# The router's logits with the weights stationary, the choice made on logits, and the first gather ahead of the branch

## The chip, the core and the metric

One core of a Trainium2 chip runs the whole program in one launch. The metric is device microseconds of one execution. Everything is fp32. Matmuls of the big layers run on operands in the fp32r format, split in two parts; the router and the experts use plain fp32 operands.

## The reference, cut to what matters

The program is two layers of three sublayers (four feed-forward, one pooling, one attention), a hybrid mixer, and at the end a mixture of experts for 256 tokens of 1024 channels. Only the last part is touched:

```
def hier_moe(h, w_rg, b_rg, w_re, b_re, w_eg, w_eu, w_ed):
    xt = h.reshape(n_tok, dm)                       # 256 x 1024
    lg = xt @ w_rg + b_rg                           # 4 groups
    grp = jnp.argmax(lg, axis=-1)
    p_grp = take_along_axis(softmax(lg), grp)
    le = (xt @ w_re + b_re).reshape(n_tok, 4, 8)    # 8 experts of each group
    le = le of the group grp
    top_p, top_i = lax.top_k(softmax(le), 2)
    gate = top_p / sum(top_p) * p_grp
    expert = grp * 8 + top_i
    ...
    yb = (silu(xb @ w_eg[e]) * (xb @ w_eu[e])) @ w_ed[e]   # per expert, on its tokens
    return sum over a token's two experts of gate * yb
```

## The kernel before, in words

Weights come from DRAM in one stream of chunks of 1.5 MB into a ring of six slots. SyncE issues chunk n as soon as chunk n-6 is used (semaphore `chunk_used`, line 236 in the loop). Each engine's program is written out by hand, and semaphores alone order the engines. TensorE's helper `mm` (line 398) issues all matmuls; an fp32 matmul stands in the trace as two instructions with a weight load each, a transpose as one.

The stages are in order: pre-norm of the experts' input, which leaves `H` (channels on partitions, 8 tiles of 128 channels x 256 tokens, VectorE line 2122); the router; a branch; the experts.

The router before. TensorE: for each half of the tokens (t) and each channel tile (k), a matmul with the tile of `H` as weights (128x128) and 36 columns of router weights as moving data, 16 matmuls in all, so the logits lie with tokens on partitions. Then 16 transposes of `H` (line 1225) into psA, which ScalarE copies to `HTOK` (line 1902), tokens on partitions. VectorE: the bias, then steps on little tiles, each waiting for the one before (`link`). `first_max` is five such steps (largest, equal, times a falling weight, largest, equal) and gives the first largest entry as one-hot. It finds the group, masks the experts' logits, subtracts the largest, and waits for ScalarE's exponentials (lines 1905, 1906, behind the copy in ScalarE's order). On the exponentials it finds the two experts `O1` and `O2`, and their sum `ASG` (line 2748) lets TensorE count, by three matmuls, each token's place in its expert's list. Meanwhile VectorE works out the gates (lines 2750 to 2757), then the places `POS` (line 2760), the longest list (lines 2761 and 2764, with TensorE's transpose 1234 between), and writes it to `most` (line 2765).

All engines read `most` and branch: to `sparse()` if no expert has over 64 tokens (it is taken here), else to `dense()`. In `sparse()` experts go in 16 pairs. A pair's selection matrix `SEL` is two compares on VectorE (line 2241); TensorE gathers the pair's tokens with it from `HTOK` (`gather`, 16 matmuls, in two halves of four channel tiles), VectorE copies each half to `XE` (line 2254); `select` turns `SEL` and picks the gates (line 1277 and two matmuls of 2 columns); then the gate and up matmuls, 64 instructions of 512 columns, read the ring and begin to free its slots. Within a pair TensorE goes on with the transposes of line 1305, the next pair's select and gather, and the down matmuls.

Filled into waits of TensorE are matmuls without use, `idle(n, w)`, each two instructions of w columns. During the router nine transfers of 0.5 MB, issued from ScalarE (line 1985), put the last three chunks of the first pair into free parts of `mem`, and one chunk goes to the ring slot that the router's weights leave.

Of the kernel before, what the change touches and what calls it, by code (L numbers as in the profile page):

```python
# [18 lines left out]
P = 128  # L19
S = 256  # L20
# [44 lines left out]
for _n, _c in [("c", 8), ("ada_b", 144), ("norm_g", 96), ("pool_b", 8), ("pool_scale", 8),  # L65
               ("norm_mix", 8), ("norm_ffn", 8), ("b_gate", 24), ("q_norm", 2), ("kv_norm", 1),
               ("conv_a", 12), ("conv_g", 48), ("qk_gain", 4), ("out_gain", 1), ("pe", 32),
               ("b_rt", 36), ("a_log", 4), ("dt", 4)]:
    COLS[_n] = (NCOL, NCOL + _c)
    NCOL += _c  # L70
# [7 lines left out]
def build(nc, stream, cols_d, ident_d, x_d, masks_d, out_d):  # L78
    ctx = ExitStack()
    with ctx:  # L80
# [304 lines left out]
        HTOK, XE = tiles(16, 2, D), tiles(18, 1, P)  # L385
        EARLY_AT = (0, 1, 2, 3, 23, 25, 14, 15, 20)
# [8 lines left out]
        def _(pe):  # L395
# [817 lines left out]
            def router():  # L1213
                c = BASE["out"] + 2
                for t in range(TT):
                    for k in range(KT):
                        pe.wait_ge(h_ready, 8 * 7 + k + 1)
                        a = 2 * SLOT + k * 36
                        last = mm(psS[:, 0, t * 36:(t + 1) * 36], H[:, k, t * P:(t + 1) * P],
                                  chunk(c, a, a + 36), start=(k == 0), stop=(k == KT - 1))  # L1220
                last.then_inc(chunk_used, 1)

                for t in range(TT):
                    for k in range(KT):
                        last = nc.tensor.transpose(psA[:, 2 * t + k // 4, (k % 4) * P:(k % 4 + 1) * P],
                                                   H[:, k, t * P:(t + 1) * P], ident)
                last.then_inc(sem("rt_htok"), 1)

                pe.wait_ge(sem("rt_asg"), 1)
                mm(psS[:, 0, 0:E], before, ASG[:, 0, :], start=True, stop=True)  # L1230
                mm(psS[:, 0, E:2 * E], before, ASG[:, 1, :], start=False, stop=False)
                mm(psS[:, 0, E:2 * E], ones, ASG[:, 0, :], start=False, stop=True).then_inc(sem("rt_cnt"), 1)
                pe.wait_ge(sem("rt_max1"), 1)
                nc.tensor.transpose(psS[0:1, 0, 256:256 + P], blk(22)[:, 128:129], ident).then_inc(sem("rt_max1t"), 1)
# [27 lines left out]
            def sparse():  # L1262


                def gather(r, p):
                    pe.wait_ge(sem("sp_sel"), r * 6 + (p + 1))
                    for b in range(2):
                        for k in range(4 * b, 4 * b + 4):
                            for t in range(TT):
                                last = mm(psG[:, b, (k % 4) * P:(k % 4 + 1) * P], HTOK[:, t, k * P:(k + 1) * P],  # L1270
                                          SEL[:, p % 2, t, :], start=(k % 4 == 0 and t == 0), stop=(t == 1))
                        last.then_inc(sem("sp_ga"), 1)
# [66 lines left out]
                def step(r, p):  # L1339
# [4 lines left out]
                    if not isinstance(r, int) or p < NP - 1:  # L1344
                        select(r, p + 1)
                        gather(r, p + 1)
                    down(r, p)

                pe.wait_ge(sem("htok_out"), 1)
                gather(0, 0)  # L1350
# [11 lines left out]
            def dense():  # L1362

                t0 = 4 * NF
                for t in range(TT):
# [12 lines left out]
                pe.wait_ge(sem("htok_out"), 1)  # L1378
# [88 lines left out]
        def _(ac):  # L1467
# [432 lines left out]
            def router():  # L1900
                ac.wait_ge(sem("rt_htok"), 1)
                A(HTOK.rearrange("p t (b n) -> p (t b) n", b=2), psA[:, :, :], ACT.Copy).then_inc(sem("htok_out"), 1)
                ac.wait_ge(sem("rt_max"), 1)

                A(blk(24)[:, 256:264], blk(24)[:, 256:264], ACT.Exp)
                A(blk(24)[:, 128:192], blk(24)[:, 128:192], ACT.Exp).then_inc(sem("rt_exp"), 1)
# [91 lines left out]
        def _(ve):  # L1998
# [232 lines left out]

            def sparse():

                def selection(r, p):

                    if p >= 2 or not isinstance(r, int):
                        ve.wait_ge(sem("sp_st"), r * 2 + (p - 1))
                    for t in range(TT):
                        a = t * E + 2 * p
                        pos = blk(22)[:, 64 + a:66 + a] if isinstance(r, int) else blk(22)[:, bass.ds(r * 4 + (64 + a), 2)]  # L2240
                        last = V.tensor_tensor(SEL[:, p % 2, t, :].rearrange("p (e s) -> p e s", e=2),
                                               iota[:, None, :].to_broadcast([P, 2, CAP]),
                                               pos[:, :, None].to_broadcast([P, 2, CAP]), ALU.is_equal)
                    last.then_inc(sem("sp_sel"), 1)
# [4 lines left out]

                def xe(r, p):  # L2250

                    for b in range(2):
                        ve.wait_ge(sem("sp_ga"), r * 4 + (2 * p + b + 1))
                        V.tensor_copy(XE[:, 4 * b:4 * b + 4, :].rearrange("p k s -> p (k s)"), psG[:, b, :])\
                            .then_inc(sem("sp_xe"), 1)
# [8 lines left out]
                def step(r, p):  # L2264
                    hidden(r, p)
                    if not isinstance(r, int) or p < NP - 1:
                        xe(r, p + 1)
# [4 lines left out]
                selection(0, 0)  # L2272
                selection(0, 1)
                xe(0, 0)
# [102 lines left out]
            def hybrid():  # L2377
# [312 lines left out]
                add_acc()  # L2690

# [4 lines left out]

            def router():
                w = blk(24)
# [370 lines left out]
```

## Time and profile before

| | us |
|---|---|
| median of 3 runs | 1949.6 (1947.92 to 1955.89) |
| the profiled execution | 1949.58, its span 1947.5 |
| TensorE matmul busy | 1832.8 (94% of the span) |
| VectorE busy | 976.4 (50%) |
| ScalarE busy | 684.1 (35%) |
| DMA, mean over the span | 248 GB/s |

Busy shares are averages over stages with different limits, and say little of a stretch of 30 us. The line numbers in rows are those of the kernel before; a matmul's line is mostly the helper's, so its tiles tell which it is: `psS<-ring,H` are the logits, `psA<-cst,H` the transposes, `psG<-mem` the gather, `psG<-cst` the idle matmuls, `psS<-ring,mem` the gate and up matmuls.

### The profile page before, as it was taken

How to read it: one execution, taken by the hardware profiler on the slowest of the kernel's cores; microseconds unless marked ns; L12 is line 12 of the kernel's file. 1: busy time of each engine (PE TensorE's matmuls, PEld its weight loads, DVE VectorE, ACT ScalarE, POOL GpSimd, SP SyncE). 2: the span in 40 equal slices, each digit the busy share in tenths (PEclk: the TensorE clock that was granted, in tenths of full speed). 3: DMA queues.
4: the chain of work that ended last, by engine and by line, in shares of the span. 5: the costliest groups of instructions: out<-in, count | busy, mean ns of one | idle time of the engine just before them, and what ended most of it. 6: DMA issues, size and time to landing. Idle time of an engine off the chain costs nothing.

```text
span 1947.5 us, 33027 instructions
## 1 busy us (share of the span) xinstructions
PE 1832.8 (94%) x13777; PEld 1505.1 (77%) x13777; DVE 976.4 (50%) x1406; ACT 684.1 (35%) x1049; POOL 21.6 (1%) x14
## 2 busy tenths in 40 slices
PE   7999999999999988999999899988888999999997
PEld 5999989999999976799998799877774543444433
DVE  3988668886855446355457775456522111111111
ACT  3444444444443335344445333455411110110101
POOL 0000000000000000000000021000000000000000
PEclk9999999999999999999998899989998999999999
DMA  9999529995664411534532222522354999999997
GB/s 394 425 365 341 190 102 374 343 346 195 270 249 173 184 55 66 195 140 184 192 132 98 98 98 98 211 95 103 138 200 189 413 426 426 424 425 425 425 425 297
DMA packets 46045, 483.46 MB, mean 248 GB/s; under 512 B 5105, under 2 KB 5233, under 8 KB 7153
## 3 DMA queue, kind: packets, MB, share of 16 engines
q1 hardware_dynamic: 44496, 476.09, 61.8%
q10 hardware_dynamic: 1440, 5.77, 0.8%
q8 instruction: 88, 1.44, 0.3%
q14 instruction: 21, 0.16, 0.0%
HBM read 480.79 MB, written 1.05 MB: 247 GB/s over the span
## 4 chain that ended last, share of the span: by engine, by line
PE 42%; DMA 8%; DVE 4%; ACT 2%; issue 1%; DVEq 0%; SPq 0%; ACTq 0%
PE psG L398 25%; PE psA L398 9%; DMA ring<-stream 8%; PE psS L398 6%; DVE parts L2089 1%; ACT parts L1505 0%; DVE mem L2403 0%; ACT mem L1866 0%; PE psS L1305 0%; DVE sg L2424 0%; DVE mem L2173 0%; PE psS L1159 0%; ACT mem L1516 0%; DVE mem L2668 0%; DVE mem L2645 0%
## 5 line engine op out<-in xcount | busy, mean ns | idle before, releaser
L398 PE MATMUL psG<-parts 128*128 128x256 f32 x6016 | 772.7, 288 | 13.0 <-issue 9.0
L398 PEld LDWEIGHTS psG<-parts 128*128 128x128 f32 x6016 | 748.1, 195 | 30.4 <-issue 24.4
L398 PE MATMUL psA<-parts 128*128 128x256 f32 x2368 | 303.2, 284 | 1.8 <-DVE parts L2260 1.6
L398 PEld LDWEIGHTS psA<-parts 128*128 128x128 f32 x2368 | 290.7, 192 | 18.1 <-issue 15.6
L398 PE MATMUL psS<-ring,mem 128*64 128x512 f32 (+1 forms) x1028 | 232.1, 598 | 20.5 <-DMA ring<-stream 17.3
L2027 DVE TENSOR_TENSOR parts<-ring,parts 128x2048 fp32r<-128x2048 f32 x80 | 183.1, 2289 | 117.6 <-ACT parts L1481 117.3
L398 PEld LDWEIGHTS psS<-ring,mem 128*64 128x64 f32 (+1 forms) x1028 | 72.7, 138 | 175.5 <-issue 132.2
L1481 ACT ACTIVATE parts<-ring 128x2048 fp32r<-128x2048 f32 x80 | 153.1, 1914 | 89.1 <-PE psA L398 88.5
L2018 DVE SCALAR_TENSOR_TENSOR mem<-ring,silc,mem 128x1536 f32<-128x1536 f32 (+1 forms) x98 | 138.8, 1417 | 2.5
L2089 DVE TENSOR_TENSOR parts<-ring,parts 128x1024 fp32r<-128x1024 f32 x76 | 95.2, 1257 | 88.8 <-ACT parts L1505 87.6
L1505 ACT ACTIVATE parts<-ring 128x1024 fp32r<-128x1024 f32 x76 | 79.9, 1053 | 139.4 <-PE psG L398 139.4
L2248 DVE TENSOR_TENSOR mem<-mem,psS 128x512 f32<-128x512 f32 x16 | 11.0, 687 | 234.0 <-ACT mem L1931 234.0
L1592 ACT ACTIVATE sg<-psG 128x256 f32<-128x256 f32 x88 | 33.8, 384 | 212.8 <-PE psG L398 212.6
L398 PE MATMUL psG<-ring,mem 128*64 128x512 f32 x480 | 106.3, 595 | 0.7 <-ACT mem L1933 0.7
L2030 DVE TENSOR_TENSOR parts<-ring,parts 128x1024 fp32r<-128x1024 f32 x80 | 97.4, 1218 | 0.0
L1931 ACT ACTIVATE mem<-psS 128x512 f32<-128x512 f32 x16 | 9.6, 598 | 233.8 <-PE psS L398 233.8
L398 PE MATMUL psG<-mem 128*128 128x128 f32 (+3 forms) x624 | 81.1, 312 | 5.1 <-ACT mem L1876 2.9
L1482 ACT ACTIVATE parts<-ring 128x1024 fp32r<-128x1024 f32 x80 | 83.3, 1042 | 0.0
L398 PEld LDWEIGHTS psG<-ring,mem 128*64 128x64 f32 x480 | 33.0, 137 | 62.7 <-issue 60.1
L2191 DVE TENSOR_TENSOR act<-sg,psG 128x256 f32<-128x256 f32 x88 | 37.0, 421 | 87.4 <-ACT sg L1592 84.3
L398 PEld LDWEIGHTS psG<-mem 128*128 128x128 f32 (+2 forms) x624 | 68.4, 189 | 12.8 <-issue 7.2
L1926 ACT ACTIVATE parts<-psG,mem 128x512 fp32r<-128x512 f32 x32 | 22.0, 687 | 147.7 <-PE psG L398 147.7
(351 smaller groups left out, 1537.9 us busy)
## 6 DMA issues: line engine op xcount, KB each, us to landing
ring<-stream SPq DMA_DIRECT2D x300, 1536.0 KB, 9.0
mem<-stream ACTq DMA_DIRECT2D x9, 512.0 KB, 7.2
X<-x_in SPq DMA_DIRECT2D x1, 1024.0 KB, 18.0
ring<-stream SPq DMA_DIRECT2D x1, 1024.0 KB, 22.3
mem<-masks ACTq DMA_DIRECT2D x1, 1024.0 KB, 4.8
x_out<-X SPq DMA_DIRECT2D x4, 256.0 KB, 2.9
ring<-stream SPq DMA_DIRECT2D x1, 512.0 KB, 23.9
cst<-consts SPq DMA_DIRECT2D x1, 304.0 KB, 2.9
```

What stands on the lines that cost most here:

```text
L398: return nc.tensor.matmul(out, lhsT, rhs, start=start, stop=stop, skip_group_check=True)
L1481: A(WG[f % 2][:, 0, :], chunk(c, 0, 2 * SLOT), ACT.Copy).then_inc(sem("hi_gu"), 1)
L1482: A(WD[t % 3][:, 0, :], chunk(c, 2 * SLOT, CHUNK), ACT.Copy).then_inc(sem("hi_dn"), 1)
L1505: A(WS[s % 3][:, 0, :], chunk(c, a, a + SLOT), ACT.Copy).then_inc(sem("slot_hi"), 1)
L1592: A(sg[:, t % 2, :], psG[:, t % 2, 0:S], ACT.Silu).then_inc(sem("silu_ready"), 1)
L1926: A(YS[:, 0, h * 512:(h + 1) * 512], psG[:, h, :], ACT.Copy, scale=GSL[:, p % 2:p % 2 + 1])\
L2018: ins = V.scalar_tensor_tensor(out, w[:, q], silc[:, k:k + 1], out, ALU.mult, ALU.add)
L2027: V.tensor_tensor(WG[f % 2][:, 1, :], chunk(c, 0, 2 * SLOT), WG[f % 2][:, 0, :], ALU.subtract).then_inc(sem("lo_gu"), 1)
L2030: V.tensor_tensor(WD[t % 3][:, 1, :], chunk(c, 2 * SLOT, CHUNK), WD[t % 3][:, 0, :], ALU.subtract).then_inc(sem("lo_dn"), 1)
L2089: V.tensor_tensor(WS[s % 3][:, 1, :], chunk(c, a, a + SLOT), WS[s % 3][:, 0, :], ALU.subtract).then_inc(sem("slot_lo"), 1)
L2191: V.tensor_tensor(act[:, f % 2, :], sg[:, f % 2, :], psG[:, f % 2, S:2 * S], ALU.mult).then_inc(sem("hidden"), 1)
L2248: V.tensor_tensor(HACT, HSIL, psS[:, 1, :], ALU.mult).then_inc(sem("sp_act"), 1)
```

## The change

Logits: the router's weights (36 columns) are stationary and `H` moves (256 columns), so the logits come out with groups and experts on partitions and tokens along the row. VectorE adds the bias there (`LGX`, 36x256), and TensorE turns the result back by two transposes of 128 tokens. The 16 transposes of `H` are spread: seven between the logits of the tiles, five behind them, four behind the two turned logits.

Choice: the experts are found on the logits, not on their exponentials, with -1e30 on those of other groups. `ASG` no longer needs ScalarE. The gates use exp of the difference of the two best logits, and are worked out behind both first selections. ScalarE loads its table for exp by a dummy activation ahead of the copy.

Ahead of the branch stand now: the selections of the first two pairs, the first pair's gather and copies. 26 idle matmuls are added, 22 ahead of the counts and 4 behind them. `POS` counts from 1, and the row of positions that it is compared with too, which takes away a step. The 36 memsets of falling weights go to the end of the mixer, ahead of the pre-norm.

```
             def router():                                  # TensorE
-                for t in range(TT):
-                    for k in range(KT):
-                        pe.wait_ge(h_ready, 8 * 7 + k + 1)
-                        last = mm(psS[:, 0, t * 36:(t + 1) * 36], H[:, k, t * P:(t + 1) * P],
-                                  chunk(c, a, a + 36), start=(k == 0), stop=(k == KT - 1))
+                for k in range(KT):
+                    pe.wait_ge(h_ready, 8 * 7 + k + 1)
+                    a = 2 * SLOT + k * 36
+                    last = mm(psS[0:36, 0, 0:S], chunk(c, a, a + 36), H[:, k, :], start=(k == 0), stop=(k == KT - 1))
+                    if k < KT - 1:
+                        token(0, k)
                 last.then_inc(chunk_used, 1)
-                for t in range(TT):
-                    for k in range(KT):
-                        last = nc.tensor.transpose(psA[:, 2 * t + k // 4, (k % 4) * P:(k % 4 + 1) * P],
-                                                   H[:, k, t * P:(t + 1) * P], ident)
+                token(0, KT - 1)
+                for k in range(4):
+                    token(1, k)
+                pe.wait_ge(sem("rt_lgx"), 1)
+                for t in range(TT):
+                    last = nc.tensor.transpose(psS[:, 0, S + t * 36:S + (t + 1) * 36], LGX[:, t * P:(t + 1) * P],
+                                               ident[0:36, 0:36])
+                last.then_inc(sem("rt_lgt"), 1)
+                for k in range(4, KT):
+                    last = token(1, k)
                 last.then_inc(sem("rt_htok"), 1)
+                idle(22, P)
                 pe.wait_ge(sem("rt_asg"), 1)
...
+                idle(4, P)
+                pe.wait_ge(sem("htok_out"), 1)
+                gather_half(0, 0, 0)
                 pe.wait_ge(sem("rt_max1"), 1)
...
+                gather_half(0, 0, 1)
...
             def sparse():                                  # TensorE
-                pe.wait_ge(sem("htok_out"), 1)
-                gather(0, 0)
+                pe.wait_ge(sem("rt_gate"), 1)
                 select(0, 0)
...
             def router():                                  # ScalarE
+                A(blk(24)[0:1, 1000:1001], eps[0:1, 0:1], ACT.Exp)
                 ac.wait_ge(sem("rt_htok"), 1)
...
                 ac.wait_ge(sem("rt_max"), 1)
-                A(blk(24)[:, 256:264], blk(24)[:, 256:264], ACT.Exp)
-                A(blk(24)[:, 128:192], blk(24)[:, 128:192], ACT.Exp).then_inc(sem("rt_exp"), 1)
+                A(EX, EX, ACT.Exp).then_inc(sem("rt_exp"), 1)
...
             def router():                                  # VectorE
-                link(V.tensor_tensor(LGT, rt, b36, ALU.add))
+                link(V.tensor_scalar(LGX, psS[0:36, 0, 0:S], col("b_rt", 0)[0:36], None, ALU.add), "rt_lgx")
+                ve.wait_ge(sem("rt_lgt"), 1)
+                lg = psS[:, 0, S:S + 72].rearrange("p (t c) -> p t c", t=2)
...
+                first_max(lg[:, :, 0:4], W4, OH, 0, 4)
+                link(V.tensor_scalar(OH, OH, 1.0, 1e30, ALU.subtract, ALU.mult))
+                for t in range(TT):
+                    last = V.tensor_tensor(LE[:, t, :].rearrange("p (g e) -> p g e", g=4),
+                                           lg[:, t, 4:36].rearrange("p (g e) -> p g e", g=4),
+                                           OH[:, t, :][:, :, None].to_broadcast([P, 4, 8]), ALU.add)
+                link(last)
+                first_max(LE, W32, O1, 1, 32)
+                link(V.scalar_tensor_tensor(T1, O1, -4e30, LE, ALU.mult, ALU.add))
                 first_max(T1, W32, O2, 4, 32)
                 link(V.tensor_tensor(ASG, O1, O2, ALU.add), "rt_asg")
+                V.tensor_tensor(EXL, lg[:, :, 0:4], Z[:, 0].to_broadcast([P, 2, 4]), ALU.subtract)
+                link(V.tensor_tensor(D2, Z[:, 4], Z[:, 1], ALU.subtract), "rt_max")
+                ve.wait_ge(sem("rt_cnt"), 1)
+                link(V.tensor_tensor(POS, ASG, psS[:, 1, 0:2 * E].rearrange("p (t e) -> p t e", t=2), ALU.mult))
+                selection(0, 0)
+                link(V.tensor_reduce(blk(22)[:, 128:129], blk(22)[:, 64:128], AX.X, ALU.max), "rt_max1")
+                selection(0, 1)
+                ve.wait_ge(sem("rt_exp"), 1)
...
+                xe(0, 0, 0)
                 ve.wait_ge(sem("rt_max1t"), 1)
...
                 link(V.tensor_copy(most[0:1, 0:1], blk(22)[0:1, 130:131]), "rt_flag")
+                xe(0, 0, 1)
```

TensorE from the logits to the first expert matmul, before (`rt_asg` is VectorE's assignment, `rt_max1` its maximum per token, `rt_flag` the value in `most`, `sp_sel` the selection, `sp_xe` the copied gather):

```order
L398 MATMUL psS<-ring,H 128x36 [waits h_ready] x16
L1225 MATMUL psA<-cst,H 128x128 x16
L398 MATMUL psS<-mem,cst 128x32 [waits rt_asg]
L398 MATMUL psS<-mem,cst 128x32 x2
L1234 MATMUL psS<-cst,mem 1x128 [waits rt_max1]
L1458 TENSOR_LOAD most [waits rt_flag]
...
L1459 COMPARE_AND_BRANCH
L398 MATMUL psG<-mem 128x128 [waits sp_sel,htok_out]
L398 MATMUL psG<-mem 128x128 x15
L1277 MATMUL psS<-cst,mem 128x128 x2
```

The same stretch of TensorE in the changed kernel, from the last tile of logits on (`rt_lgx` is the biased logits, `rt_gate` the gates; ahead of these rows seven pairs of a 36x256 matmul and a transpose):

```order
L399 MATMUL psS<-H,ring 36x256 [waits h_ready]
L1220 MATMUL psA<-cst,H 128x128 x5
L1235 MATMUL psS<-cst,mem 128x36 [waits rt_lgx]
...
L1220 MATMUL psA<-cst,H 128x128 x4
L399 MATMUL psG<-cst 128x128 x22
L399 MATMUL psS<-mem,cst 128x32 [waits rt_asg]
...
L399 MATMUL psG<-cst 128x128 x4
L399 MATMUL psG<-mem 128x128 [waits sp_sel,htok_out]
...
L1251 MATMUL psS<-cst,mem 1x128 [waits rt_max1]
L399 MATMUL psG<-mem 128x128 x8
...
L1478 COMPARE_AND_BRANCH
L1296 MATMUL psS<-cst,mem 128x128 [waits rt_gate]
```

The gather has moved ahead of the branch, in two halves around the transpose of the maximum, and 22 idle matmuls stand between the transposes and the counts.

VectorE from the assignment to the first copy of the gather, before (2748 is the assignment, 2760 the places, 2765 the flag, 2241 the selections, 2254 the copies):

```order
L2748 TENSOR_TENSOR mem<-mem 128x64 [waits dve_step]
L2750 TENSOR_TENSOR mem<-mem 128x2 [waits rt_asg]
...
L2752 RECIPROCAL mem<-mem 128x2 [waits dve_step]
...
L2757 TENSOR_TENSOR mem<-mem 128x64 [waits dve_step]
L2760 TENSOR_TENSOR mem<-mem,psS 128x64 [waits rt_cnt,rt_gate]
L2761 TENSOR_REDUCE mem<-mem 128x1 [waits dve_step]
...
L2765 CAST most<-mem 1x1 [waits dve_step]
...
L2820 COMPARE_AND_BRANCH
L2241 TENSOR_TENSOR mem<-cst,mem 128x128 x4
L2254 COPY mem<-psG 128x512 [waits sp_ga] x2
```

And in the changed kernel (2757 is the assignment, 2763 the places, 2257 a selection's compare, 2780 the flag, 2265 the copies):

```order
L2757 TENSOR_TENSOR mem<-mem 128x64 [waits dve_step]
...
L2763 TENSOR_TENSOR mem<-mem,psS 128x64 [waits rt_cnt,rt_max]
L2257 TENSOR_TENSOR mem<-cst,mem 128x128 [waits dve_step]
...
L2765 TENSOR_REDUCE mem<-mem 128x1
L2257 TENSOR_TENSOR mem<-cst,mem 128x128 [waits rt_max1]
...
L2769 TENSOR_REDUCE mem<-mem 128x2 [waits rt_exp]
...
L2775 TENSOR_TENSOR mem<-mem 128x64 [waits dve_step]
L2265 COPY mem<-psG 128x512 [waits sp_ga,rt_gate]
...
L2780 CAST most<-mem 1x1 [waits dve_step]
L2265 COPY mem<-psG 128x512 [waits sp_ga,rt_flag]
...
L2836 COMPARE_AND_BRANCH
```

The gates' steps, which stood between the assignment and the places, now stand behind the selections, and the flag is written between the two copies.

## Rows read from the trace of the kernel before

**Rows 1.** The page's first line, of the whole span.

```profile
span 1947.5 us, 33027 instructions
```

**Rows 2.** Chain of waits in order of time: start us, us, what ran.

```profile
1410.89 27.91 PE psA L398 x128
...
1445.98 6.13 PE psS L398 x32
1452.11 3.48 PE psA L1225 x16
1455.61 1.88 ACT mem L1902
1457.50 1.28 ACT L1905
...
1465.80 0.55 DVEq L2819
...
1467.46 6.64 PE psG L398 x32
...
1474.87 13.98 PE psS L398 x64
...
1584.93 14.16 DMA ring<-stream
...
1702.82 2.03 issue
```

**Rows 3.** Windows: busy time of each engine (count), granted clock, DMA share, GB/s.

```profile
1445.90:1449.00 3.10, 3.02 (x18) 2.36 (x17) 3.09 (x39) 0.00 (x0) 0.00 (x0) 1.00 0.88 301
1449.00:1452.10 3.10, 3.10 (x19) 3.10 (x19) 0.14 (x12) 0.00 (x0) 0.00 (x0) 0.58 1.02 408
1456.00:1458.00 2.00, 0.00 (x0) 0.00 (x0) 0.00 (x0) 1.98 (x2) 0.00 (x0) 0.92 1.03 426
1460.00:1462.00 2.00, 0.00 (x0) 0.00 (x0) 1.75 (x8) 0.00 (x0) 0.00 (x0) 0.50 0.27 111
1462.50:1467.40 4.90, 1.86 (x7) 1.43 (x7) 3.12 (x17) 0.00 (x0) 0.00 (x0) 0.50 0.00 0
1530.00:1543.00 13.00, 13.00 (x64) 4.22 (x60) 0.75 (x1) 0.41 (x1) 0.00 (x0) 1.00 1.02 433
```

**Rows 4.** Timeline of the router: start us, us, engine, instruction [idle before <- releaser].

```profile
1438.40 2.19 PEld L398 LDWEIGHTS psG<-cst 128*128 128x128 f32 x18
...
1443.69 0.55 DVE L2061 RECIPROCAL st<-st 128x64 f32<-128x64 f32 x1 [2.32 <-ACT st L1485]
...
1445.44 3.22 DVE L2122 SCALAR_TENSOR_TENSOR H<-X,cols,psS 128x256 f32<-128x256 f32 x8 [1.20 <-PE psS L398]
...
1448.61 0.49 DVE L2713 MEMSET mem<- 128x1 f32 x32
...
1452.42 0.16 DVE L2723 TENSOR_REDUCE mem<-mem 128x2 f32<-128x8 f32 x1
...
1459.25 0.16 DVE L2743 TENSOR_REDUCE mem<-mem 128x2 f32<-128x8 f32 x1 [3.85 <-ACT mem L1906]
...
1462.28 0.22 DVE L2748 TENSOR_TENSOR mem<-mem 128x64 f32<-128x64 f32 x1
...
1462.56 1.49 PE L398 MATMUL psS<-mem,cst 128*128 128x32 f32 x6 [6.99 <-DVE mem L2748]
...
1464.30 0.22 DVE L2760 TENSOR_TENSOR mem<-mem,psS 128x64 f32<-128x64 f32 x1
...
1465.62 0.14 DVE L2765 CAST most<-mem 1x1 int32<-1x1 f32 x1
...
1466.82 0.90 DVE L2241 TENSOR_TENSOR mem<-cst,mem 128x128 f32<-128x128 f32 x4 [1.06 <-issue]
...
1474.13 0.69 DVE L2254 COPY mem<-psG 128x512 f32<-128x512 f32 x1 [2.19 <-PE psG L398]
```

**Rows 5.** Groups by line and shape, window 1689 to 1720: the gather of a later pair.

```profile
L398 PE MATMUL psG<-mem 128*128 128x128 f32 x32 | 3.8, 278 | 0.0
```

## What the change will do to the time

> **What bounds the kernel now.** The change touches one short stretch, so I read three views: the page's first line for the whole, the chain of waits for what sets the end, and the windows and the timeline for that stretch. The profiled execution took 1949.58 us, its span 1947.5 [rows 1]; 2.1 us lie around the span and stay. Its own time equals the median of the runs (1949.6), so a shift of the span carries over one to one.
>
> The chain [rows 2] shows two regimes. From 1474.87 on the experts run: the first pairs are set by TensorE, but from 1584.93 the chain steps through waits of some 14 us on the weight stream, and the DMA engines are full at 433 GB/s [rows 3]. That looks as if TensorE and VectorE before it did not matter. They do: between the transfers that end at 1460.7 (27% of the window 1460 to 1462) and the first expert matmul the DMA moves nothing (its row reads 0 GB/s) [rows 3]. The ring and the side buffers are full, and nobody frees a slot. The stream starts again only when the first pair's gate-and-up matmuls start; call that moment T0, now 1474.87. Everything after T0 depends on T0 alone, so each microsecond off the router comes off the end.
>
> The stretch from H to T0, 1445.98 to 1474.87 (28.9 us), is a single chain over TensorE, ScalarE and VectorE: 32 logit matmuls 6.13, 16 transposes 3.48, ScalarE's 2048-column copy 1.88, a table load 1.28, then the exponentials; VectorE sits 3.85 us until they are there [rows 2, 4]; then VectorE's small steps, the counts, the branch, 6.64 us of gather. The granted clock is 0.58 from 1449 and 0.50 later [rows 3]: one step from 2.4 to 1.2 GHz, at about 1449.5 (0.5 us at full and 2.6 at half make the mean of 0.58 over 3.1), after 3.5 us of matmuls with 36 moving columns. The gather ran at 1.2 GHz; the same 32 instructions in a later pair take 3.8 us [rows 5].
>
> **The change, part by part.** Pitches that I use: a 128x256 fp32 instruction 27.91/128 = 0.22 us [rows 2]; a 128x128 one at full clock 2.19/18 = 0.12 us [rows 4], the gather 3.8/32 = 0.12 [rows 5], at half clock 16 transposes in 3.48 = 0.22 [rows 2]. One fp32 matmul is two instructions, one transpose is one. VectorE: 64-column steps from 1459.25 to 1462.28 are one short one (0.20) and eleven of (3.03-0.20)/11 = 0.26 [rows 4]; the 8-column ones 0.20.
>
> 1. *Logits.* 16 instructions of 256 columns, 7 transposes between them: 16x0.22 + 7x0.12 = 4.3, and some 0.15 for the last one's tail. VectorE makes H at 3.22/8 = 0.40 a tile [rows 4], faster than the 0.56 that TensorE takes per tile, so H does not gate. End 1450.4, against 1452.1.
> 2. *Bias and turn.* The bias add reads 36x256 from PSUM. Not in the trace; between the small steps (0.2) and the 512-column copy (0.69) [rows 4]; scaled by columns 0.43. Then two transposes and back: 0.06 to start, 0.12 for the first, 0.4 for the second (the counts' 1.49 less five pitches of 0.22), 0.1 back. New: 1450.4+0.05+0.43+0.65 = 1451.5 for the first group step, which now starts at 1452.42. Gain 0.9. The 36 memsets (0.49 for 32 of them, now from 1448.61) would stand in front of this; they move to where VectorE idles 2.32 us before the reciprocal at 1443.69 [rows 4], which hides them. Without that cover they cost 0.6.
> 3. *Choice on logits.* Group 5x0.20, mask 0.20, two adds 0.33, then 1.28, 0.26, 1.28, 0.22 = 4.6 to the assignment: 1456.1, against 1462.50. The wait for ScalarE (3.85) and the group steps of the old softmax are gone. The table load moves behind the last early DMA issue and ahead of the copy, and only ten columns are exponentiated; the result is wanted at 1459.4, about 2.5 us after it is there. If the table had to be loaded twice, it would still be there.
> 4. *Warm-up matmuls.* This is what is late next. Behind the two turned logits stand 4 transposes and idle(22), 44 instructions: 50x0.12 = 6.0 from 1450.9, to 1456.9. The assignment is there at 1456.1, so the counts wait 0.8 in TensorE's queue; VectorE waits for them. Counts start 1456.9, before 1462.56: gain 5.7.
> 5. *Counts and position.* At full clock 5x0.12+0.35 = 0.95 (before 1.49). VectorE's multiply starts 1457.9; before 1464.30, since the gates stood in front. Gain 6.4. The gates' steps move behind both selections, 1.4 us to about 1460.85, just under the first gather half.
> 6. *Selection and gather ahead of the branch.* Multiply 0.26, two selection steps 0.5 (0.90 for four): 1458.7. Here the flag, the branch (VectorE: 1465.76 to 1466.82, 1.06) and the maximum used to stand between; now the gather starts at 1458.75 instead of 1467.46, gain 8.7. idle(4), 0.96, ends at about 1458.6 and hides under it. Halves: 16x0.12 each and one transpose: last issued 1462.7, result 1462.9. Copy 0.69: 1463.6 (before 1474.82). Gain 11.2 on this branch.
> 7. *Branch and select.* VectorE: first copy 1460.9 to 1461.6, flag 1462.1, ahead of the second copy. TensorE then branches and does the first pair's two transposes and four 2-column instructions, 6x0.12. Before, these lay under the copy; now they lie behind. The cost of TensorE's branch is not seen apart: from below 0 beyond the gather; from above the 2.03 us "issue" at the loop's end at 1702.82 [rows 2]; VectorE's own 1.06 [rows 4] is the nearest. With 1.06 counted from 1462.7: 1463.8, select 0.75: T0 = 1464.5. With 0: 1463.7 (the copy ends then); with 2.03: 1465.6.
>
> By the Trainium skill (TensorE: Matmul & The Clock Gate, opening table), TensorE's queue is 64 deep. If its sequencer runs that far ahead, the branch starts at the flag, and T0 would be about 1463.9; no run here shows that.
>
> Sum: 1474.87 - 1464.5 = 10.4, bounds 9.2 to 11.2. Nothing is added behind T0; the stream sees the same full ring (all landed by 1460.7 in either kernel, since the one chunk that the router frees and the nine early ones are the same bytes). 1949.6 - 10.4 = 1939.2.
>
> **Rivals.**
> *The clock drops as before, at about 1449.5, and comes back as before* (for: it is the same transposes, and TensorE waits at the turn; against: 256-column matmuls at 0.22 leave no such gaps as 36-column ones, and idle(22) fills the wait). Then six tiles of logits are done at full, the rest at half: 1451.1. From 1451.6 the 50 instructions run at 0.22 until the clock is back, as it was in the window 1456 to 1458 [rows 3]: some 22 by 1456.4, the other 28 at 0.12 to 1459.8. The counts are 2.9 later than in the forecast and the rest follows: T0 1467.4, time 1942.1.
> *The slower one: the clock falls as the logits start and stays.* Then 16x0.43+7x0.22 = 8.4, logits at 1454.4; the warm-up becomes the bound, 50x0.22 = 11 from 1455.0 to 1466.0, 3.4 later than the counts are now. Counts issued by 1467.3, idle(4) eight more to 1469.1, 33 gather instructions to 1476.4, branch 1.06, select 6x0.22 = 1.3: T0 1478.7, time 1953.4. It decides from the point where the clock falls at 1449.5 and does not return: counts at 1462.6, T0 by the same steps 1475.3, just above today's, since idle(22) at half clock eats all that VectorE saved. Against: from 1445.9 to 1449 the clock was 1.0 [rows 3].
> The row that bears on both: in 1456 to 1458 the clock granted is 0.92 with TensorE empty [rows 3]; it rose after the 16 transposes, which were all it had done since 1452.1.
> The Trainium skill (TensorE: Matmul & The Clock Gate, Part 4: PE-mode transpose) says that transposes don't count as TensorE activity and the full clock doesn't engage for them. By that rule the 17 transposes now mixed in are holes, and the time goes to the two rivals. This trace disagrees with it: 0.92 behind 16 transposes.
> *The gain is swallowed by the stream*: the experts are DMA-bound from 1584.93, so an earlier start only waits longer. For: the 14 us waits. Against: 0 GB/s for the 14 us before T0. It would give 1949.6.
> *A dearer branch*: 2.03 instead of 1.06, T0 1465.6, time 1940.3.
>
> **Numbers.** Forecast 0.72, inside it 1937 to 1941.5; dearer branch 0.12; clock down and back 0.08; swallowed 0.04; slower rival 0.04. The range takes in the forecast, the dearer branch, the clock that returns, and a spread between runs like that of before (1947.92 to 1955.89, mostly upward): 1936.3 to 1944.0. About 0.5% (9.7 us, the line 1939.85) is what a measurement of this kernel tells from no change. The forecast lies only 0.65 inside it: of its 0.72 about 0.48 is faster than the line, and a cheaper branch is in that; of the dearer branch 0.04. Faster 0.52, within 0.46, slower 0.02 (half of the slower rival with an upward run).
>
> **What would show it.** Right: granted clock 1.0 from 1446 to T0; first group step near 1451.5; the counts starting when the idle matmuls end and not when the assignment is ready; the gather in two parts of about 1.9 us; T0 at 1464 to 1465.6; and the whole pattern from T0 to the end unchanged, 1947.5 - 1474.87 = 472.6 us of span behind it. Wrong: a clock of 0.5 in any of it (then step 4 fails first), a branch on TensorE of over 2 us, or a distance from T0 to the end that has grown.

## The result and the profile after

The changed kernel takes 1941.37 us in the median of 11 runs (1937.07 to 1946.73); the kernel before, in 11 runs too, 1951.35 (1947.64 to 1956.3). The ratio is 0.995, 95% interval 0.994 to 0.996, about 10 us. The forecast of 1939.2 started from 1949.6, the median of three runs, so 1.75 of the 2.2 us between forecast and result is the kernel before, and 0.4 the change. The profiled execution took 1942.88 us, its span 1940.9. That is 6.6 us of span less than before [rows 1], not 10, and the stretches tell why.

The chain of waits of the changed kernel, in order of time (start us, us, what ran):

```profile
1413.38 27.91 PE psA L399 x128
...
1448.47 0.62 PE psS L399 x2
...
1456.30 4.91 PE psG L399 x44
1461.21 0.59 PE psS L399 x6
1461.81 0.97 PE psG L399 x8
1462.81 2.02 PE psG L399 x16
1464.94 1.79 PE psG L399 x16
1466.73 0.41 issue
1467.14 0.43 PE psS L1296 x2
1467.57 14.25 PE psS L399 x68
...
1577.90 14.08 DMA ring<-stream
```

Set beside [rows 2] it falls into three pieces. Up to the first logit: 1448.47, before 1445.98, 2.5 us *later*, in code that both kernels share but for the 36 memsets, and all of it is there at the first row already (1413.38, before 1410.89). From there to T0, the first expert matmul, at 1467.84: 19.4 us, before 28.9. From T0 to the end: 1940.9 - 1467.84 = 473.1, before 472.6. So the change is worth 9.5 us in its own stretch, and a pair of executions can show more or less than that, here 6.6, since the start of the logits lies anywhere from 1442.4 to 1452.7 in the thirteen profiles of this study. From T0 to the end they differ by 0.9 at most, so that wandering makes up nearly all of how their spans differ once T0 is taken from the first logit. All comparisons below therefore go by the time from the first logit instruction, written +x; a difference of rounded times can be 0.01 off.

| us from the first logit | before | after | forecast |
|---|---|---|---|
| last logit done, bias add starts | +6.17 | +6.35 | +4.5 |
| first group step | +6.44 | +7.35 | +5.5 |
| assignment done | +16.52 | +11.94 | +10.1 |
| counts start (first weight load) | +16.58 | +12.47 | +10.9 |
| place step | +18.32 | +13.44 | +11.9 |
| gather starts | +21.48 | +14.34 | +12.8 |
| T0 | +28.89 | +19.37 | +18.5 |

The windows of the changed kernel (columns as in [rows 3]):

```profile
1448.40:1454.80 6.40, 6.33 (x24) 2.22 (x25) 2.76 (x8) 1.49 (x2) 0.00 (x0) 1.00 0.95 360
1454.80:1460.90 6.10, 6.10 (x54) 5.89 (x55) 4.68 (x23) 2.07 (x2) 0.00 (x0) 1.00 1.04 428
1460.90:1466.70 5.80, 5.77 (x50) 5.42 (x49) 3.50 (x16) 0.02 (x1) 0.00 (x0) 1.00 0.37 153
1466.00:1468.00 2.00, 1.59 (x15) 1.39 (x15) 0.69 (x1) 0.06 (x1) 0.00 (x0) 1.00 0.00 0
1524.00:1536.00 12.00, 12.00 (x58) 3.86 (x54) 0.17 (x1) 0.00 (x0) 0.00 (x0) 1.00 1.02 434
```

The granted clock is 1.00 all through the router, the DMA still falls silent before T0 (0 GB/s from 1466), and it is full again later, as before [rows 3].

The timeline of the changed kernel, around the logits and around the branch (start us, us, engine, line, operation, then in brackets the idle time ahead and what ended it):

```profile
1448.47 0.14 PEld L399 LDWEIGHTS psS<-H,ring 128*36 128x36 f32 x2 [0.27 <-DVE H L2140]
1448.47 0.62 PE L399 MATMUL psS<-H,ring 128*36 128x256 f32 x2
1449.03 0.14 PEld L1220 LDWEIGHTS psA<-cst,H 128*128 128x128 f32 x1 [0.41 <-issue]
1449.03 0.33 PE L1220 MATMUL psA<-cst,H 128*128 128x128 f32 x1
1449.29 0.14 PEld L399 LDWEIGHTS psS<-H,ring 128*36 128x36 f32 x2
...
1460.18 0.23 DVE L2757 TENSOR_TENSOR mem<-mem 128x64 f32<-128x64 f32 x1
...
1460.94 0.75 PEld L399 LDWEIGHTS psS<-mem,cst 128*128 128x128 f32 x6
...
1461.91 0.22 DVE L2763 TENSOR_TENSOR mem<-mem,psS 128x64 f32<-128x64 f32 x1 [1.24 <-PE psS L399]
...
1465.85 0.14 DVE L2780 CAST most<-mem 1x1 int32<-1x1 f32 x1
1466.83 0.69 DVE L2265 COPY mem<-psG 128x512 f32<-128x512 f32 x1 [0.84 <-PE psG L399]
1467.13 0.20 PEld L1296 LDWEIGHTS psS<-cst,mem 128*128 128x128 f32 x2 [0.59 <-issue]
```

A tile of logits takes 0.81 us (1448.47 to 1449.29), not 0.56: the load for the transpose starts only 0.56 after the pair of matmuls began, when they are nearly through, with the load side idle for 0.41. The branch is the opposite case, cheaper than forecast: from the flag (1465.85 + 0.14 = 1465.99) to TensorE's first instruction behind the branch (1467.13) it is 1.14 us, of which only 0.41 lie behind the last gather matmul (1466.73). The rest ran while the gather was still in TensorE's queue.

### The profile page after: what moved, and what is told of

The parts are those of the page before. It is cut to its first block, busy times and chain, and to the rows that moved or that the text cites. A ratio compares the mean times of both kernels' runs of the same rounds, so it can differ in the third digit from the quotient of the medians.

```text
span 1940.9 us, 33097 instructions
## 1 busy us (share of the span) xinstructions
PE 1835.1 (95%) x13815; PEld 1504.3 (78%) x13815; DVE 975.0 (50%) x1399; ACT 683.8 (35%) x1049; POOL 21.6 (1%) x14
## 4 chain that ended last, share of the span: by engine, by line
PE 40%; DMA 9%; DVE 5%; ACT 2%; issue 1%; DVEq 0%; SPq 0%; ACTq 0%
PE psG L399 24%; DMA ring<-stream 9%; PE psA L399 9%; PE psS L399 6%; DVE parts L2107 1%; DVE mem L2418 1%; ACT parts L1524 0%; ACT mem L1885 0%; PE psS L1324 0%; DVE sg L2439 0%; PE psS L1160 0%; DVE mem L2191 0%; ACT mem L1535 0%; DVE mem L2416 0%; DVE mem L2683 0%
```

## Experiments

**All logits first** (six runs). The transposes leave the gaps between the logits; 28 idle instructions instead of 44.

```
                     last = mm(psS[0:36, 0, 0:S], chunk(c, a, a + 36), H[:, k, :], start=(k == 0), stop=(k == KT - 1))
-                    if k < KT - 1:
-                        token(0, k)
                 last.then_inc(chunk_used, 1)
-                token(0, KT - 1)
-                for k in range(4):
-                    token(1, k)
+                for k in range(5):
+                    token(0, k)
...
-                for k in range(4, KT):
+                for k in range(5, KT):
+                    token(0, k)
+                for k in range(KT):
                     last = token(1, k)
...
-                idle(22, P)
+                idle(14, P)
```

> The changed kernel with its transposes taken out from between the logits: eight logit matmuls first, five transposes behind them, then the two turned logits, then the other eleven transposes, and idle(14) in place of idle(22). Counted from the first logit instruction; the changed kernel has the first group step at +7.35, the counts at +12.47, T0 (first expert matmul) at +19.37 us. Theory A, a matmul behind a transpose and a transpose behind a matmul each wait until the array is empty (0.81 us a tile instead of 0.56): without the seven changes of kind the logits run at 0.22 a piece or at the pace of H, bias add at +3.8, first group step at +4.8 to +4.9, counts at +9.6, T0 at +16.4 to +16.9, so 2.5 to 3 us less than the changed kernel, about 1938.5 where that one has 1941.4. Theory B, a transpose is simply dear by 0.25 us wherever it stands: the eleven transposes behind the turn take 11x0.36 = 4 us, the counts are at about +12, T0 at +19, no gain.

The timeline of this kernel, TensorE and the two VectorE steps that it feeds:

```profile
1446.92 3.64 PE L399 MATMUL psS<-H,ring 128*36 128x256 f32 x16
...
1450.49 0.77 PE L1220 MATMUL psA<-cst,H 128*128 128x128 f32 x5
1450.60 0.48 DVE L2734 TENSOR_SCALAR mem<-psS,cols 36x256 f32<-36x256 f32 x1 [1.00 <-PE psS L399]
...
1451.43 1.42 PE L1220 MATMUL psA<-cst,H 128*128 128x128 f32 x11
1451.61 0.17 DVE L2740 TENSOR_REDUCE mem<-psS 128x2 f32<-128x8 f32 x1 [0.53 <-PE psS L1232]
...
1456.23 0.85 PE L399 MATMUL psS<-mem,cst 128*128 128x32 f32 x6 [0.26 <-DVE mem L2756]
...
1463.03 1.51 PE L399 MATMUL psS<-ring,mem 128*64 128x512 f32 x6
```

Bias add at +3.69, group step +4.70, counts +9.32, T0 +16.12: 3.25 us less than the changed kernel. The sixteen narrow logit instructions run at 0.22 a piece, the transposes in a row at 0.11. Theory B falls: no transpose is dear by itself. The median is 1937.11 us, the ratio to the kernel before 0.9939 (0.9926 to 0.9952). T0 also comes near to another limit here: the DMA still moves 139 GB/s from 1461.5 to 1462.0 and 12 GB/s from 1462 to 1463, so the early transfers have landed only some 1.3 us ahead of T0 (1463.03); in the changed kernel that is some 4.7 us, before 14. The distance from T0 to the end is still 472.4.

**Wide weights** (one run).

```
-                    last = mm(psS[0:36, 0, 0:S], chunk(c, a, a + 36), H[:, k, :], start=(k == 0), stop=(k == KT - 1))
+                    last = mm(psS[:, 0, 0:S], chunk(c, a, a + P), H[:, k, :], start=(k == 0), stop=(k == KT - 1))
```

> The changed kernel with 128 columns of the chunk as the logits' weights instead of 36 (rows 36 to 127 of the result are not used by anything). Theory A (change of kind): the pitch of a tile stays at 0.81 us, T0 at +19.4. Theory C (a narrow weight load of 36 columns keeps the next load from being taken ahead): pitch falls to 0.56, bias add at +4.5 instead of +6.35, T0 at +18.1 or where the idle matmuls let it, since those end then at +10.9.

The timeline of the kernel with wide weights, TensorE and its load side, at its first logits (start us, us, engine, line and operation):

```profile
1448.85 0.30 PEld L399 LDWEIGHTS psS<-H,ring 128*128 128x128 f32 x2 [0.26 <-DVE H L2140]
1448.85 0.70 PE L399 MATMUL psS<-H,ring 128*128 128x256 f32 x2
1449.17 0.14 PEld L1220 LDWEIGHTS psA<-cst,H 128*128 128x128 f32 x1
1449.39 0.27 PE L1220 MATMUL psA<-cst,H 128*128 128x128 f32 x1
1449.39 0.30 PEld L399 LDWEIGHTS psS<-H,ring 128*128 128x128 f32 x2
```

The same order, the same changes of kind, three and a half times the weights: 0.54 a tile (1448.85 to 1449.39). The transpose's load now starts 0.32 after the matmuls did, inside them. Theory A falls, theory C stands. The bias add is at +4.54 (expected +4.5), T0 at +17.42, 1.95 less than in the changed kernel, and earlier than the +18.1 expected. What about a narrow load holds back the wide one no run shows; only 36 and 128 columns were tried.

**Turned by plain matmuls** (one run), in `token`:

```
-                    return nc.tensor.transpose(psA[:, 2 * t + k // 4, (k % 4) * P:(k % 4 + 1) * P],
-                                               H[:, k, t * P:(t + 1) * P], ident)
+                    return mm(psA[:, 2 * t + k // 4, (k % 4) * P:(k % 4 + 1) * P],
+                              H[:, k, t * P:(t + 1) * P], ident, start=True, stop=True)
```

> The changed kernel with the 16 transposes of H done as plain fp32 matmuls against the identity, two instructions each. Theory A (change of kind, matmul to transpose mode): no change of kind is left among them, so a tile takes 2x0.22+2x0.12 = 0.67 us, bias add near +5.3. Theory C (narrow weights): the stall stays, 0.81+0.12 = 0.93 us a tile, bias add near +7.2. The other nine turns cost 9x0.12 = 1.1 us more in either case.

TensorE's load side at this kernel's first logits:

```profile
1444.94 0.14 PEld L399 LDWEIGHTS psS<-H,ring 128*36 128x36 f32 x2 [0.26 <-DVE H L2140]
1445.49 0.30 PEld L399 LDWEIGHTS psA<-cst,H 128*128 128x128 f32 x2 [0.41 <-issue]
1445.91 0.14 PEld L399 LDWEIGHTS psS<-H,ring 128*36 128x36 f32 x2
```

0.97 a tile (1444.94 to 1445.91), bias add at +7.46, T0 +21.52. With no transpose left among the logits the stall is there (load side idle for 0.41), so by this too it goes with the weights' width (36 beside 128) and not with the mode. The size was close to theory C's 0.93.

**No idle matmuls** (one run).

```
-                idle(22, P)
...
-                idle(4, P)
```

> The changed kernel without its 26 idle matmuls. Theory K (they hold the clock): TensorE is empty from about +7.8 to +11.9, the granted clock falls to 0.5 before or in the counts, they take 1.3 to 1.5 instead of 0.75, a gather half 3.3 to 3.5 instead of 2.0, T0 at about +22.5, 3 us later. Rival: the clock would stay by itself, and the idle matmuls only delay the counts: T0 at +18.8, 0.5 us earlier.

Its windows from behind the group step to T0 (columns as in [rows 3]):

```profile
1453.00:1457.00 4.00, 0.10 (x1) 0.11 (x1) 3.45 (x19) 1.66 (x1) 0.00 (x0) 0.94 1.05 435
1457.00:1459.30 2.30, 1.38 (x6) 1.25 (x6) 0.88 (x6) 0.21 (x1) 0.00 (x0) 0.50 0.96 403
1459.30:1463.10 3.80, 3.71 (x17) 3.66 (x18) 1.71 (x10) 0.00 (x0) 0.00 (x0) 0.50 0.08 32
1463.10:1466.00 2.90, 2.74 (x24) 2.56 (x22) 1.71 (x4) 0.00 (x0) 0.00 (x0) 0.96 0.00 0
```

The clock fell behind a stretch in which TensorE had next to nothing to do (0.10 of 4.00 us); counts took 1.49, the first gather half 3.75. But it was back for the second half (2.05), and the counts had started 0.5 sooner, so T0 came at +21.15, 1.8 later and not 3. Theory K is right, its price was too high.

**Gather behind the branch** (one run). TensorE's part, with four idle matmuls more behind the maximum's transpose; on VectorE both selections, the gates and the two copies likewise move from `router()` to the head of `sparse()`, and the maximum and the flag follow the places directly.

```
             def router():
-                pe.wait_ge(sem("htok_out"), 1)
-                gather_half(0, 0, 0)
                 pe.wait_ge(sem("rt_max1"), 1)
...
-                gather_half(0, 0, 1)
+                idle(4, P)
...
             def sparse():
+                pe.wait_ge(sem("htok_out"), 1)
+                gather_half(0, 0, 0)
+                gather_half(0, 0, 1)
                 pe.wait_ge(sem("rt_gate"), 1)
```

> The changed kernel with the first two selections, the first gather, its copies and the gates put back behind the branch; logits, choice and idle matmuls stay (the four ahead of the gather stand ahead of the branch). Times from the first logit instruction; the changed kernel has its position step at +13.44 and T0 at +19.37. If the move ahead of the branch is worth what stood between: maximum, its transpose and the flag 1.5 us, branch 1.06 to 1.14, two selection steps 0.5, gather 4.0, copy 0.7 from +13.7: T0 at +21.4, 2 us later. If the new order only exchanged one wait for another (branch and select behind the gather), T0 stays within 0.3 of +19.4.

Its timeline around the branch, VectorE and TensorE:

```profile
1461.74 0.14 DVE L2775 CAST most<-mem 1x1 int32<-1x1 f32 x1
1462.95 0.90 DVE L2258 TENSOR_TENSOR mem<-cst,mem 128x128 f32<-128x128 f32 x4 [1.06 <-issue]
...
1463.59 3.81 PE L399 MATMUL psG<-mem 128*128 128x128 f32 x32 [1.37 <-DVE mem L2258]
...
1467.43 0.69 DVE L2266 COPY mem<-psG 128x512 f32<-128x512 f32 x1 [1.03 <-PE psG L399]
...
1468.18 1.08 PE L399 MATMUL psS<-ring,mem 128*64 128x512 f32 x4 [0.22 <-DVE mem L2266]
```

T0 at 1468.18, +21.27: 1.90 later, as expected. Here VectorE's branch (1.06) stands in full in the chain, as it did before.

**H as weights, the rest of the change kept** (one run).

```
+                for t in range(TT):
+                    for k in range(KT):
+                        last = mm(psS[:, 0, t * 36:(t + 1) * 36], H[:, k, t * P:(t + 1) * P],
+                                  chunk(c, a, a + 36), start=(k == 0), stop=(k == KT - 1))
+                last.then_inc(chunk_used, 1)
+                for t in range(TT):
+                    for k in range(KT):
+                        last = token(t, k)
...
+                link(V.tensor_tensor(lg, psS[:, 0, 0:72].rearrange("p (t c) -> p t c", t=2), b36, ALU.add))
```

> The changed kernel with the logits as before (H tiles as weights, 36 moving columns, 16 matmuls, then 16 transposes), the rest kept: choice on logits, idle(22), gather ahead of the branch. If only the layout's matmul count matters: logits end at +6.1 as before, choice from +6.4 instead of +7.35, a gain of 0.9 that the idle matmuls take away. If the 36-column stream drops the clock as in the kernel before: granted clock 0.5 from about 3 to 4 us after the first logit, the transposes take 3.5 us instead of 1.9, idle(22) runs partly at 0.22 a piece and ends at +15 or later instead of +12.4, T0 at +21.5 to +24.

Its windows over the logits, the transposes and what follows them (columns as in [rows 3]):

```profile
1444.00:1448.00 4.00, 3.92 (x25) 3.08 (x24) 3.22 (x8) 0.05 (x1) 0.00 (x0) 1.00 0.93 314
1448.00:1452.00 4.00, 4.00 (x23) 4.00 (x23) 0.41 (x3) 1.43 (x2) 0.00 (x0) 0.58 1.02 417
1452.00:1456.00 4.00, 4.00 (x23) 4.00 (x22) 3.45 (x18) 1.02 (x1) 0.00 (x0) 0.56 1.08 441
1456.00:1460.00 4.00, 4.00 (x38) 4.00 (x37) 0.57 (x4) 0.95 (x2) 0.00 (x0) 1.00 0.88 370
```

The logits end no later than in the changed kernel (group step +6.53 against +7.35), but the clock falls under them. The 16 transposes take 3.65, the idle matmuls start at +9.47, and the counts behind them only at +14.64, although the assignment was done at +11.11; T0 +21.46, at the early end of what was expected. So undoing the layout costs 2.1 us, and by the clock and the transposes in a row, not by more matmuls. Part of the 2.1 is that the 22 idle matmuls, partly at half clock here, hold the counts back by 3.5; the old layout with fewer of them was not run.

**The kernel before with idle matmuls alone** (ten runs).

```
                 last.then_inc(sem("rt_htok"), 1)
+                idle(26, P)
...
                 mm(psS[:, 0, E:2 * E], ones, ASG[:, 0, :], start=False, stop=True).then_inc(sem("rt_cnt"), 1)
+                idle(4, P)
...
                 nc.tensor.transpose(psS[0:1, 0, 256:256 + P], blk(22)[:, 128:129], ident).then_inc(sem("rt_max1t"), 1)
+                idle(6, P)
```

> The kernel before with idle matmuls alone: 26 behind the transposes, 4 behind the counts, 6 behind the maximum's transpose, no other part of the change. Logits and transposes keep their times (the clock falls ahead of the idle matmuls). If the clock is worth what its pitches say: back at full at about +10.5, counts 0.75 to 0.95 instead of 1.49, gather 4.0 instead of 6.6, select 0.7 instead of 1.1: T0 at +25.3 to +26 instead of +28.89, 3 us off the end, ratio 0.9985. Rival, that the clock only falls again in the waits between counts and gather: T0 within 0.5 of +28.9, ratio 1.000.

A window of its trace and its gather:

```profile
1460.00:1464.00 4.00, 4.00 (x37) 4.00 (x37) 1.41 (x7) 2.26 (x4) 0.00 (x0) 1.00 0.79 330
1470.50 3.81 PE L398 MATMUL psG<-mem 128*128 128x128 f32 x32 [0.93 <-DVE mem L2244]
```

The clock is 1.00 in every window of 4 us from 1460 to 1472; counts 0.85 instead of 1.49 [rows 4], gather 3.81 instead of 6.64 [rows 2]. T0 +26.75, 2.15 less than before, and later than the +25.3 to +26 expected: the logits took 6.90 here instead of 6.13, since the clock fell some 1.4 us into them and not 3.5. The ratio 0.9987 (0.9977 to 0.9997) fits the 0.9985 expected and shuts out the rival's 1.000 only narrowly.

**A delay ahead of T0** (one run).

```
+                for i in range(8):
+                    link(V.tensor_copy(blk(21)[:, 0:512], blk(21)[:, 512:1024]))
                 xe(0, 0, 1)
```

> The changed kernel with eight chained copies of 512 columns (0.69 us each) on VectorE ahead of the second gather copy, into a tile that nothing needs yet. T0 moves by eight times 0.7 or less, since some lies under the second gather half: from +19.37 to about +24. If all behind T0 hangs rigidly on T0: 472.4 to 473.3 us of span behind T0 as in the other runs, although the weight stream sets the pace there. If the stream swallowed shifts: the distance shrinks by the delay, to about 468.5.

Its timeline around T0, the eight added copies in the first row:

```profile
1459.93 3.66 DVE L2782 COPY mem<-mem 128x512 f32<-128x512 f32 x8
...
1463.62 0.69 DVE L2265 COPY mem<-psG 128x512 f32<-128x512 f32 x1
1464.36 0.20 PEld L399 LDWEIGHTS psS<-ring,mem 128*64 128x64 f32 x4 [2.73 <-DVE mem L2265]
```

In this chain a copy from SBUF came every 0.46, where one from PSUM takes 0.69, so T0 is only 2.6 later, +21.99. Its span is 1936.9, so 472.5 us lie behind T0. The distance over all thirteen profiles is 472.4 to 473.3, with T0 anywhere from +16.0 to +28.9; a swallowed 2.6 would lie far outside. Half a microsecond could hide in that spread.

**Side by side**: the changed kernel, logits first, and logits first with the flag ahead of the gates, whose edit to VectorE is this (on TensorE the maximum's transpose goes ahead of the gather, and idle(3) stands for idle(4); the flag's lines no longer stand between the copies):

```
-                selection(0, 0)
                 link(V.tensor_reduce(blk(22)[:, 128:129], blk(22)[:, 64:128], AX.X, ALU.max), "rt_max1")
+                selection(0, 0)
                 selection(0, 1)
+                ve.wait_ge(sem("rt_max1t"), 1)
+                link(V.tensor_reduce(blk(22)[0:1, 130:131], psS[0:1, 0, 0:P], AX.X, ALU.max))
+                link(V.tensor_copy(most[0:1, 0:1], blk(22)[0:1, 130:131]), "rt_flag")
```

> The changed kernel itself, to be timed beside the next two. T0 at +19.4 from the first logit instruction with 472.4 to 473.3 us behind it as before; 1941 us or so, ratio 0.995.

> The kernel with all logits ahead of the transposes, unchanged, beside the changed kernel on one chip. Its T0 came 3.25 us earlier in the trace (+16.12 against +19.37), so its time should be 3.2 us lower than that of the changed kernel, ratio to the kernel before 0.9935 against 0.995. If it was luck of one profile: the two are equal within 1 us.

> The kernel with all logits first, and the flag written ahead of the gates: the maximum goes ahead of the first selection, its transpose ahead of the gather, three idle matmuls instead of four. If TensorE's branch (seen at 1.1 us from the flag, running while the gather's matmuls are still in its queue) is all that stands between gather and select, select follows the gather without the 0.3 us gap, but the gather itself starts 0.2 to 0.3 later since the maximum is now ahead of it and the gates come later: T0 at +16.0 to +16.2, no change that a timing can tell. If the branch held more than its gap: T0 below +15.8.

| | T0 in its trace | median us (runs) | ratio to before |
|---|---|---|---|
| changed kernel | +19.29 | 1939.87 (5) | 0.9936 (0.9924 to 0.9949) |
| logits first | +16.12 | 1939.45 (6) | 0.9934 (0.9921 to 0.9947) |
| and flag early | +16.05 | 1938.57 (6) | 0.9929 (0.9917 to 0.9941) |

The traces repeat to 0.1 us; the times don't separate the three: the two medians that were to lie 3.2 apart lie 0.4 apart. Three us are 0.15%, and the intervals are 0.25% wide. Over all runs of this study the means are 1941.1 for the changed kernel (16 runs) and 1938.6 for logits first (12 runs), 2.4 apart where the traces say 3.2, but most of those runs were not made side by side. Whether a measurement of whole runs would give all 3.2 stays open. The early flag takes the 0.3 us gap behind the gather and starts the gather 0.27 later, nothing in sum, as expected.

## Why the prediction was right, and where it was not

The forecast was 1939.2 in a range of 1936.3 to 1944.0; the measured gain is 10 us in the runs and 9.5 in the stretch, against 10.4. The mechanism held: T0 sets the end, and a delay put ahead of it is passed on (the delay experiment); what lies behind T0 grew by 0.4. T0 itself, at +19.37, lies in the +18.0 to +19.6 that the prediction named, but the first group step does not (+7.35, named +5.5). By the steps:

1. *Logits: wrong.* The step took 0.56 a tile from pitches of 128-wide loads [rows 2, 4] and put them beside 36-wide ones. It is 0.81, since a load of 128 columns is not taken ahead over matmuls with 36; the logits ended 1.85 us later than forecast, no sooner than before. With 128-wide weights for the logits a tile takes 0.54, and with the shapes kept apart all 16 logit instructions take 3.64.
2. *Bias and turn: right in size* (0.48 and 0.53 against 0.43 and 0.65). With step 1 the forecast gain of 0.9 is a loss of 0.9. The memsets ran in VectorE's wait (idle ahead of the reciprocal 1.61 instead of 2.32), as argued.
3. *Choice on logits: right.* From the first group step to the assignment 4.59 us against 4.6; before, that stretch took 10.08, of which 3.85 was the wait for ScalarE [rows 4]. It is the largest single part.
4. *Warm-up matmuls: right.* They end after the assignment (1460.41), and the counts wait 0.5 for them, forecast 0.8. Both the idle matmuls and the choice start from the two turned logits, so late logits move both alike; the wait is shorter because the 50 instructions took 5.5 (1455.40 to 1460.94) instead of 6.0.
5. *Counts and position: right.* From the first load of the counts to the place step 0.97, forecast 1.0.
6. *Selection and gather ahead: right.* Worth 1.9 us by the undo, and the gates hid under the first half (done 1464.64; the half's copy starts at 1464.94).
7. *Branch and select: too dear by 0.65.* I counted 1.06 from the end of the gather. It runs from the flag, and most of it under the gather: 0.41 showed. The Trainium skill (TensorE: Matmul & The Clock Gate, opening table) gives TensorE's queue 64 entries; the 1.14 us from flag to select with gather matmuls running in them agrees with it, and the T0 that the prediction worked out from it was 0.6 sooner than the one it forecast.

From the place step to T0 it took 5.9, forecast 6.6. That and the shorter wait of step 4 took back 1.0 of the 1.85 that step 1 lost. So the 9.5 came nearer to 10.4 than the worst step was to its own value; that the misses had opposite signs was luck. Without the miss of step 1 (all logits first) the stretch gains 12.8, more than the upper bound of 11.2.

The two rivals on the clock were out: it stayed at 1.00. Against the Trainium skill's rule on transposes (TensorE: Matmul & The Clock Gate, Part 4: PE-mode transpose) stands mainly the row that the prediction quoted, a clock back up behind 16 transposes [rows 3]. The changed kernel adds little to it, since its transposes take only 0.26 of each 0.81 among the logits, and with H as weights the clock was back only when idle matmuls had run behind the 16 transposes. (The prediction counted 17 transposes; there are 18, 16 of `H` and two of the logits.)

That the layout with 36 moving columns brings the clock down was argued before, and the kernel with H as weights shows it: 0.58 in the window 1448 to 1452, with the rest of the change in place. That it is not the missing mix with transposes is shown by the kernel with all logits first, where the clock is 1.00 throughout.

How the 9.5 us divide, by undoing one part at a time: layout 2.1, idle matmuls 1.8, gather ahead of the branch 1.9. That leaves 3.75 for the choice on logits and the smaller steps, which were not undone by themselves. The parts overlap, so this remainder is not a measurement of the choice; the stretch from group step to assignment became 5.5 shorter (step 3).

## What to carry to other kernels

If a long stage that is bound by transfers starts from full buffers, look at what frees the first buffer; before it every microsecond counts, however full the DMA engines are later. That holds as long as the buffers are full by then; the kernel with all logits first has some 1.3 us of it left, and no run goes beyond. Don't alternate weight loads as narrow as these (36 columns) with loads of 128 on TensorE; do all of one shape and then all of the other, or widen the narrow ones. An idle matmul that holds the clock also holds the queue, so its number belongs to one layout and has to be set anew with the next. Where the gain is near the spread of the runs, find a fixed event in both traces and measure from there.

## What the runs showed of the hardware that I had not expected

- Behind two instructions with 36 columns of weights a load of 128 columns starts 0.56 us after the pair began, behind two with 128 columns 0.32 us; a tile of two 256-column instructions and a transpose takes 0.81 and 0.54 us. With narrow weights and the transpose done as a plain matmul: 0.97.
- TensorE's branch overlaps its queued matmuls: 1.14 us from the flag, 0.41 of it visible.
- The clock came back in the middle of a stretch at half clock where TensorE was busy with nothing but a gather of 128-column matmuls: first half 3.75 us, second 2.05.
- A 512-column copy on VectorE takes 0.43 us out of SBUF (one every 0.46 in the chain of eight) and 0.69 out of PSUM.
- Code ahead of the router that is the same but for 36 memsets ended anywhere in a span of 10 us from one profile to the next.
